# Broadcasting the gate rows by one-hot matmuls instead of a DMA round trip, and the last output waits of SyncE moved ahead of its branches

## What is computed

```
def mlstm_block(carry, inp):
    C0, n0, m0 = carry
    q, k, v, ig, lf = inp
    bcum = jnp.cumsum(lf, axis=-1)
    inter = bcum + m0[..., None]
    dmat = jnp.where(tri, bcum[..., :, None] - bcum[..., None, :] + ig[..., None, :], -jnp.inf)
    m = jnp.maximum(inter, jnp.max(dmat, axis=-1))
    w_intra = jnp.exp(dmat - m[..., None])
    w_inter = jnp.exp(inter - m)
    s = jnp.einsum('bhtd,bhsd->bhts', q, k) * w_intra
    num = w_inter[..., None] * jnp.einsum('bhtd,bhde->bhte', q, C0) + jnp.einsum('bhts,bhse->bhte', s, v)
```

## Time and profile before

| | us |
|---|---|
| median of 3 runs | 867.1 |
| the runs | 865.81, 867.10, 867.84 |
| the profiled run | 867.84 |
| its span | 866.1 |
| TensorE busy | 843.3 (97%) |
| VectorE busy | 587.9 (68%) |
| ScalarE busy | 472.0 (54%) |
| GpSimd busy | 93.2 (11%) |

### The profile page before, as it was taken

One profiled execution on the slowest core, in us unless ns is written; L12 is line 12 of the kernel. 1 busy time (PEld: TensorE's weight loads), 2 busy tenths in 40 slices (PEclk: granted clock), 3 DMA queues, 4 the chain that ended last, 5 costly groups with the idle time before them and its releaser, 6 DMA issues. The chain is left out here.

```text
span 866.1 us, 12955 instructions
## 1 busy us (share of the span) xinstructions
PE 843.3 (97%) x5145; PEld 767.9 (89%) x5145; DVE 587.9 (68%) x817; ACT 472.0 (54%) x638; POOL 93.2 (11%) x153
## 2 busy tenths in 40 slices
PE   6999999999999999999999999999999999999995
PEld 5999989999999998999999998887888888888883
DVE  5665487773445536686655556378899889899893
ACT  4654477753433234454333335427778678767763
POOL 3302111020011011000000000010002210310410
PEclk9999999999999999999999999969999999999998
DMA  9748633334344435345446454369999999999980
GB/s 269 224 152 269 192 124 110 110 120 129 121 134 134 146 122 171 110 135 173 133 145 218 147 194 147 127 202 337 365 355 352 371 381 387 359 371 388 370 306 17
DMA packets 100387, 186.61 MB, mean 215 GB/s; under 512 B 5668, under 2 KB 71488, under 8 KB 100320
## 3 DMA queue, kind: packets, MB, share of 16 engines
q1 hardware_dynamic: 95280, 171.47, 57.7%
q0 software_dynamic: 4240, 12.59, 4.4%
q10 hardware_dynamic: 800, 1.66, 0.5%
HBM read 178.55 MB, written 7.93 MB: 215 GB/s over the span
## 5 line engine op out<-in xcount | busy, mean ns | idle before, releaser
L1377 DVE TENSOR_TENSOR w_r<-arena,w_r 128x2048 fp32r<-128x2048 f32 x96 | 216.7, 2285 | 28.6 <-ACT w_r L992 28.5
L1368 DVE TENSOR_TENSOR unit_r<-arena,unit_r 128x2048 fp32r<-128x2048 f32 x63 | 144.8, 2299 | 134.0 <-ACT unit_r L981 133.8
L587 PE MATMUL pj<-xn_r,unit_r 128*128 128x320 f32 x1536 | 234.2, 311 | 0.7 <-issue 0.7
L587 PEld LDWEIGHTS pj<-xn_r,unit_r 128*128 128x128 f32 x1536 | 225.5, 188 | 4.4 <-issue 3.9
L889 PE MATMUL pj<-w_r,xg 128*128 128x512 f32 x768 | 192.2, 401 | 0.2 <-ACT xg L1221 0.2
L992 ACT ACTIVATE w_r<-arena 128x2048 fp32r<-128x2048 f32 x96 | 180.5, 1913 | 1.1 <-DMA arena<-in_w_exp_up 0.9
L889 PEld LDWEIGHTS pj<-w_r,xg 128*128 128x128 f32 x768 | 142.9, 190 | 31.2 <-issue 0.3
L981 ACT ACTIVATE unit_r<-arena 128x2048 fp32r<-128x2048 f32 x63 | 120.1, 1907 | 23.8 <-PE pj L587 20.0
L918 PE MATMUL pj<-w_r,hidT 128*128 128x512 f32 x384 | 93.4, 392 | 0.7 <-ACT hidT L1234 0.6
L918 PEld LDWEIGHTS pj<-w_r,hidT 128*128 128x128 f32 x384 | 71.8, 188 | 17.3 <-issue 1.0
L587 PE MATMUL pj<-br_r,unit_r 128*128 128x320 f32 x384 | 59.6, 311 | 0.0
(11 more groups left out here) (360 smaller groups left out, 815.2 us busy)
## 6 DMA issues: line engine op xcount, KB each, us to landing
arena<-in_w_in SPq DMA_DIRECT2D x40, 1024.0 KB, 5.3
arena<-in_w_exp_gate SPq DMA_DIRECT2D x64, 512.0 KB, 4.6
arena<-in_w_exp_up SPq DMA_DIRECT2D x64, 512.0 KB, 6.2
arena<-in_w_exp_down SPq DMA_DIRECT2D x64, 512.0 KB, 5.3
arena<-in_w_mem_v SPq DMA_DIRECT2D x4, 1024.0 KB, 5.8
arena<-in_w_br_mem SPq DMA_DIRECT2D x4, 1024.0 KB, 5.0
arena<-in_w_br_mlstm SPq DMA_DIRECT2D x4, 1024.0 KB, 4.9
arena<-in_w_br_gmlp SPq DMA_DIRECT2D x4, 1024.0 KB, 5.0
```

What stands on the lines that cost most here:

```text
L587: last = mm(bank_of(s)[0:out_rows, 0:out_cols], l, r, start=k == 0, stop=k == len(pairs) - 1)
L1368: v.tensor_tensor(unit_r[n % RING][:, 1, :], ringw[:, n % RING, :], unit_r[n % RING][:, 0, :], ALU.subtract).then_inc(u_lo, 1)
L1377: v.tensor_tensor(w_r[u % NS][:, 1, :], raw_w[u % NS], w_r[u % NS][:, 0, :], ALU.subtract).then_inc(m_lo, 1)
```

## The change

Two edits. First, the broadcast. A tile sel (4 partitions, 4 x 128) is filled by GpSimd at the start with a memset and a select: its block h has ones in partition h and zeros elsewhere. The step `bc` becomes a step of ring "ms": TensorE multiplies sel's block of head h with rb in fp32, which puts row h of rb into all 128 partitions of a PSUM bank, 385 columns. VectorE reads its five operands from that bank instead of from rbb, and releases the bank with the last. The write to memory, the read back, and the waits for both are gone, and with them the tiles rbb and spread_rows. Second, SyncE's four waits for the output scatters of the first level stand ahead of `sp.If(need >= 1)` and no longer behind all branches.

```
--- before.py
+++ after.py
@@ -101,7 +101,7 @@
         for c in (2 * u, 2 * u + 1):
             step("mq", c, ring="pj", eng="A", unit=n, last=c % 2 == 1)
             if c < H:
-                step("bc", c, ring=None, eng=None)
+                step("bc", c)
 
 
     ka = lambda h: (step("ka", h, 0), step("ka", h, 1))
@@ -306,9 +306,9 @@
         pT = take(2, 2, T)
         prows = at(B0 + 2 * D, 128)
         srows = at(B0 + 2 * D + 128, 128)
+        sel = at(B0 + 6 * D, H, 128)
         rb = at(B0 + 6 * D + H * 128, T + TS + 1)
         wif = at(B0 + 6 * D + H * 128 + 392, KC, 128)
-        rbb = at(B0 + 8 * D, H, T + TS + 1)
         off[0] = B0
         gn_g, gn_b = at(B0, D), at(B0 + D, D)
         mix_r = rounded("mix_r", B0, 2, KC, T)
@@ -408,7 +408,6 @@
         slot_token = sb("slot_token", [128, G], U32)
         slot_out = sb("slot_out", [128, G], U32)
         gpk = sb("gpk", [128, KC])
-        spread_rows = nc.dram_tensor("gate_rows", (H, T + TS + 1), FP32, kind="Internal").ap()
         x_rows = nc.dram_tensor("x_rows", (T, D), FP32, kind="Internal").ap()
 
         pj = ctx.enter_context(nc.psum_tensor("pj", [128, 4, 512], FP32))
@@ -430,7 +429,6 @@
         dchain = sem("dve_chain")
         achain = sem("act_chain")
         s_g1, s_g2, s_g3, s_g4 = sem("gates_abs"), sem("gates_log"), sem("gates_rows"), sem("gates_exp")
-        s_rbw, s_rbb = sem("gate_rows_written"), sem("gate_rows_spread")
         s_wexp, s_wt, s_wbcin = sem("weights_exp"), sem("weights_masked"), sem("weights_arg")
         s_cachek, s_cachev = [sem("cache_k0"), sem("cache_k1")], [sem("cache_v0"), sem("cache_v1")]
         s_nmx, s_exp, s_prob = sem("neg_max"), sem("probs_exp"), sem("probs_ready")
@@ -565,6 +563,8 @@
             sp.wait_ge(s_s1out, 16 * H)
             sp.wait_ge(s_nout, 32)
             sp.wait_ge(s_gvout, 16)
+            for k in range(G):
+                sp.wait_ge(m_yout[k], 16)
             with sp.If(need >= 1):
                 with sp.Fori(1, LEVELS) as lv:
                     with sp.If(need >= lv):
@@ -574,8 +574,6 @@
                 with sp.If(need >= lv):
                     for k in range(G):
                         sp.wait_ge(m_yout[k], 16 * lv + 16)
-            for k in range(G):
-                sp.wait_ge(m_yout[k], 16)
 
 
         @block.tensor
@@ -704,6 +702,8 @@
                         for q, r in enumerate((R_A, R_IG, R_F)):
                             c0 = (i * 3 + q) * H
                             last = tr(b[0:n, c0:c0 + H], rows[0:H, r, t0:t0 + n], ident[0:H, 0:H])
+                elif kind == "bc":
+                    last = mm(b[:, 0:T + TS + 1], sel[0:H, a[0], :], rb[0:H, :], start=True, stop=True)
                 elif kind == "wsT":
                     pe.wait_ge(s_ws, 16)
                     for g in range(H):
@@ -1459,14 +1459,11 @@
                     dve.wait_ge(*done("cols"))
                 elif kind == "bc":
                     h, = a
-                    if h == 0:
-                        dve.wait_ge(s_rbb, 16)
-                    r = rbb[:, h, :]
-                    v.tensor_scalar(wt[:, h, 0:256], r[:, 0:256], cols[:, 0, 0, h:h + 1], 0.0, ALU.add, ALU.min)
-                    v.tensor_scalar(wt[:, h, 256:384], r[:, 128:256], cols[:, 1, 0, h:h + 1], 0.0, ALU.add, ALU.min)
-                    v.tensor_scalar(wt[0:64, h, 384:WTW], r[0:64, TP:T], cols[0:64, 2, 0, h:h + 1], 0.0, ALU.add, ALU.min).then_inc(s_wbcin, 1)
-                    v.tensor_scalar(wbc[:, h, 0:TS], r[:, T:T + TS], QSCALE, None, ALU.mult)
-                    v.tensor_copy(wbc[:, h, TS:TS + 1], r[:, T + TS:T + TS + 1])
+                    v.tensor_scalar(wt[:, h, 0:256], b[:, 0:256], cols[:, 0, 0, h:h + 1], 0.0, ALU.add, ALU.min)
+                    v.tensor_scalar(wt[:, h, 256:384], b[:, 128:256], cols[:, 1, 0, h:h + 1], 0.0, ALU.add, ALU.min)
+                    v.tensor_scalar(wt[0:64, h, 384:WTW], b[0:64, TP:T], cols[0:64, 2, 0, h:h + 1], 0.0, ALU.add, ALU.min).then_inc(s_wbcin, 1)
+                    v.tensor_scalar(wbc[:, h, 0:TS], b[:, T:T + TS], QSCALE, None, ALU.mult)
+                    v.tensor_copy(wbc[:, h, TS:TS + 1], b[:, T + TS:T + TS + 1]).then_inc(free, 1)
                 elif kind == "paramsync":
                     dve.wait_ge(s_mnl, 3)
                     for k in range(4):
@@ -1820,7 +1817,10 @@
             link(g.memset(iog[64:128, 2, :], -1.0))
             g.iota(tokf[:, :, :], pattern=[[128, 3], [-NO_ROW, 2]], base=0, channel_multiplier=1, allow_small_or_imprecise_dtypes=True)
             link(g.memset(before[:, :], 1.0))
-            g.affine_select(out=before[:, :], in_=before[:, :], compare_op=ALU.is_gt, fill=0.0, base=0, pattern=[[1, 128]], channel_multiplier=-1).then_inc(s_const, 1)
+            g.affine_select(out=before[:, :], in_=before[:, :], compare_op=ALU.is_gt, fill=0.0, base=0, pattern=[[1, 128]], channel_multiplier=-1)
+            link(g.memset(sel[0:H, :, :], 0.0))
+            g.affine_select(out=sel[0:H, :, :], in_=sel[0:H, :, :], compare_op=ALU.not_equal, fill=1.0, base=0, pattern=[[-1, H], [0, 128]], channel_multiplier=1).then_inc(s_const, 1)
+
             pool.wait_ge(s_const, 2)
 
             def pair_samples(dst, x_r):
@@ -1865,11 +1865,6 @@
                     pool.wait_ge(*done("wsT"))
                     g.affine_select(out=wsT[:, :, :], in_=wsT[:, :, :], compare_op=ALU.is_ge, fill=0.0, base=0,
                                     pattern=[[0, H], [1, 128]], channel_multiplier=-1).then_inc(s_wsT, 1)
-                elif kind == "gates_exp":
-                    pool.wait_ge(s_g4, 1)
-                    pool.dma_start(spread_rows, rb[0:H, :]).then_inc(s_rbw, 16)
-                    pool.wait_ge(s_rbw, 16)
-                    pool.dma_start(rbb[:, :, :].rearrange("p h t -> p (h t)"), spread_rows.rearrange("h t -> (h t)").partition_broadcast(128)).then_inc(s_rbb, 16)
                 elif kind == "cols":
                     pool.wait_ge(s_g3, 1)
                     pool.dma_start(O["mlstm_m_prompt"][0, 0, :].rearrange("(h a) -> h a", a=1), rows[0:H, R_MM, TP - 1:TP]).then_inc(s_mout, 16)
```

More of the change, by code:

```diff
@@ L1867, in _ @@
                                     pattern=[[0, H], [1, 128]], channel_multiplier=-1).then_inc(s_wsT, 1)
[L1868 to L1872, removed]
                 elif kind == "cols":
```

1 line of the change is left out of this document (removed).

## The result

| | before | changed |
|---|---|---|
| median of 5 runs each, us | 866.59 | 871.37 |
| the runs, us | 864.36 to 867.84 | 870.60 to 873.70 |
| profiled run, us | 867.84 | 870.42 |
| its span, us | 866.1 | 868.7 |

In these medians the changed kernel is slower by 4.8 us. The ratio is 1.0063, with a 95% interval of 1.0047 to 1.0079. It goes by more runs than the table: 22 of the changed kernel are on record, 869.94 to 874.20 us, with a median of 871.8. The forecast was 870.4 with a range of 868.0 to 873.0, and 3.3 us slower.

The account below looks back on a forecast made before the run. The prediction took TensorE, busy 843.3 of 866.1 us, to bound the kernel. Removed stall -0.66, selector matmuls +2.83 and SyncE's exposed jump +1.1 sum to +3.3 us on a median of 867.1: 870.4, range 868.0 to 873.0.

Parts of the forecast that it names:

- TensorE sets the pace, and what is added to it costs its length: Whole span: TensorE busy 843.3 of 866.1 us, so an added instruction in the middle costs its own length.
- rival C: TensorE's waits before 533 and 191 absorb up to 2.0 us of its delay, giving 868.4; chance 0.11.
- The selector matmuls: Four fp32 matmuls of 128x385 added on TensorE between projection groups, 0.71 us each, +2.83 us, from 2.6 up to 3.2.
- its own sign: Prediction wrong if key transposes shift under 1.5 or over 3 us, or SyncE's jump takes under 1.8 or over 4.8.
- The stall of 0.66 us: TensorE's wait near 85, behind VectorE's and ScalarE's wait for the spreading DMA; removing it gains 0.66 us.
- the slack: Next weight unit rounded by 82.2, wanted by TensorE only near 86.9: 4.7 us to spare, nothing late next.
- VectorE's reads, GpSimd's start, the earlier outputs: PSUM reads in 20 small operations, memset and select in the first 5 us, outputs issued about 4 us earlier: no cost.
- The tail: End of span: SyncE's 2.9 us jump now follows the last landing, its drain 1.1 us behind GpSimd's: +1.1 us.
- A: End of span: SyncE's jump takes under 1.8 us, its target fetched during the wait, and stays hidden; 869.3, chance 0.16.
- B: End of span: SyncE's jump costs 4.8 us as at 837, +3.0 there, 872.3 in all; chance 0.14.
- The sum: Whole run: -0.66 + 2.83 + 1.1 = +3.3 us, from the median of 867.1 to 870.4; chance 0.55.
- D, the clock: Between 560 and 600: shifted work loses less of TensorE's clock, making the kernel faster, 865.3; chance 0.04.

## Why the prediction was right, and where its terms were off

- **TensorE sets the pace, and what is added to it costs its length.** Held: the shift of 4.06 us at the key transposes (0.83 of it from ahead of the change) is still 4.06 at the router matmul (533.48 before, 537.54 now), behind both waits that rival C rested on. C is rejected.
- **The selector matmuls: the term that was mis-sized.** The sum had 4 x 0.71 = 2.83 us, at most 3.2; measured 4 x 1.03 = 4.11. The row it was scaled from, the attention scores, has 128 partitions like its neighbours. The bound of 0.1 us for a change of form and shape was an estimate from rows of which none changes to a few partitions; two changes cost 0.38 us. By its own sign the prediction failed in this step: it called itself wrong if the key transposes shifted by over 3 us, and the stretch alone grew by 3.2. The direction and the path were right, the size of this term was not.
- **The stall of 0.66 us.** Its chain was read rightly, and the slack that should follow was there: 5.3 us where 4.7 were forecast (the prediction's own terms give 87.2 and not 86.9 for when TensorE wants the unit, so 5.0). But one profile was taken for the kernel: the same wait was 0, 0, 0.66 and 3.78 us in four executions, and in the last the clock made 6.6 us of it. The gain from removing it was nothing in two of the four and large in one.
- **VectorE's reads, GpSimd's start, the earlier outputs at nothing.** Held. The gate loads started 1.2 us later (5.61 for 4.37), and the gate matmul at 45.36 did not wait.
- **The tail.** Forecast +1.1 us from a jump of 2.9. In the six profiles with the moved waits and the full length of code the jump took 2.5 to 2.7 us and the tail 3.1 to 3.4, where the other eight have 2.3 to 2.5: +0.9 for the changed kernel. A (hidden) and B (4.8 us) are both rejected. The prediction took GpSimd's drain as 5.37 us from its start; in all fourteen profiles it ends 2.0 to 2.2 us behind the last landing, and that is what hides a jump.
- **The sum.** 4.1 for the matmuls and 1.0 for the tail give 5.1 less what the stall would have been; the broadcast alone measured 4.0 in the medians, the waits alone 1.5 and both 4.8. The forecast of 3.3 fell short by the matmuls' 1.3 us and by what it took for a stall that is often not there, and its range held the time. That 870.4 lies within 1.0 us of the median has a part of luck: the median that it started from, 867.1 of three runs, was 0.5 us above that of five.
- **D, the clock.** It did vary: the profile after made up 2.3 us by it between the change and the tail. But it varies in both kernels, and did not decide the sign.

## What to carry to other kernels

A DMA round trip that hides behind other engines costs the busiest engine nothing; one-hot matmuls on that engine cost their full time every run. When a short stall comes from such a trip, take a second profile before you count on it, and look first whether its consumer can stand later in the order: that took the stall to zero, even with a trip of 13.7 us, and added nothing, though the median did not get measurably better. And a wait moved from behind a branch to ahead of it exposes the jump: with 290 instructions to pass it took 2.6 us here, of which all but 0.9 hid behind GpSimd's drain.

## What the runs showed of the hardware that I had not expected

- Between matmuls that contract over 128 partitions, an fp32 matmul over 4 costs 0.38 us more (1.03 for 0.65). In the trace neither its weight load nor the next is taken ahead. Zero padding to 128 partitions removes both.
- Full busy time did not keep TensorE's clock: 3.04 us of matmuls over 4 partitions, without a gap, were followed by a granted clock of 0.53; padded, 1.00. One profile of each.
- A stall of 3.78 or 4.47 us was followed by some 5 us at the lower level, so it cost 6.6 and 7.5 us. A stall of 0.66 us left the clock at 1.00.
- The trip through memory took 8.7 to 13.4 us in four executions of the same instructions. The read back of 770 KB took 4.5 to 5.2 us when it was issued ahead of a 1 MB load on another queue, and 6.8 to 7.7 when behind it.
- SyncE's jump took 4.8 to 5.2 us while the last expert loads were moving, and 2.5 to 2.7 us with the queues idle. Over a short piece of code it took 0.2 us, and no packet of an instruction queue was moved for it.
